# A four-layer hybrid decoder step: the residual chunks' scaled copy dropped, the first stage reordered, the final norm taken in feature layout

## The reference, cut to what matters

```python
for i in range(DEPTH):                       # mixers: gated MLP, linear attention, block attention, gated MLP
    x = x + mixer_i(rms_norm(x, norm_mix[i]))
    x = x + swiglu(rms_norm(x, norm_ffn[i]), w_up[i], w_down[i])
y = rms_norm(x, norm_final)

def rms_norm(x, g):
    return x * rsqrt(mean(x * x, axis=-1) + EPS) * g
```

## Time and profile before

| | |
|---|---|
| median of 3 runs | 1685.19 us (1681.47 to 1689.21) |
| profiled execution's own time | 1688.18 us |
| its span | 1686.4 us |
| PE busy | 1568.3 us, 93% |
| DVE busy | 1122.1 us, 67% |
| ACT busy | 794.2 us, 47% |
| mean granted TensorE clock | 0.972 of full |

### The profile page before, as it was taken

The page is one execution under the profiler, slowest core; times in us unless marked ns, Lnnn a source line. Parts: engine busy times, 40 slices in busy tenths (PEclk is TensorE's granted clock), DMA queues, the critical chain, the costliest instruction groups (busy, mean ns, idle before and its releaser), DMA issues.

```text
span 1686.4 us, 33530 instructions
## 1 busy us (share of the span) xinstructions
PE 1568.3 (93%) x12471; PEld 1517.4 (90%) x12471; DVE 1122.1 (67%) x1691; ACT 794.2 (47%) x1279; POOL 174.1 (10%) x168
## 2 busy tenths in 40 slices
PE   6999999999989779999987589999999999999995
PEld 5999999999879569999977459999999999999995
DVE  5578757665665867676557955666666786676643
ACT  4566445444435545444333345444355754354432
POOL 1000010000311400000126400000210001200000
PEclk9999999999999979999999799999999999999998
DMA  5454555554535724554578643555554445555551
GB/s 182 153 172 131 173 176 176 188 184 163 176 125 197 232 84 163 186 174 163 201 253 309 228 152 103 190 181 169 180 189 162 150 153 186 177 175 176 188 174 61
DMA packets 265123, 293.19 MB, mean 174 GB/s; under 512 B 6108, under 2 KB 256276, under 8 KB 265022
## 3 DMA queue, kind: packets, MB, share of 16 engines
q1 hardware_dynamic: 260252, 278.04, 49.3%
q0 software_dynamic: 4192, 13.66, 2.4%
q10 hardware_dynamic: 578, 0.08, 0.0%
HBM read 283.51 MB, written 8.25 MB: 173 GB/s over the span
## 4 chain that ended last, share of the span: by engine, by line
PE 71%; DVE 12%; DMA 5%; ACT 4%; issue 4%; POOL 1%; SPq 1%; DVEq 1%; ACTq 0%; POOLq 0%
PE banks L471 22%; PE banks L473 21%; PE banks L475 21%; DVE wlo L445 4%; ACT whi L437 2%; DMA raw<-in_w_down 2%; DVE xl L593 1%; DVE xg L587 1%; PE banks L958 1%; DMA raw<-in_w_in_c 1%; PE banks L1448 1%; DVE x L579 1%; DMA raw<-in_w_in_a 1%; DVE sc L1919 1%; PE banks L949 1%
## 5 line engine op out<-in xcount | busy, mean ns | idle before, releaser
L445 DVE TENSOR_TENSOR wlo<-raw,whi 128x1024 fp32r<-128x1024 f32 (+1 forms) x480 | 604.5, 1265 | 328.9 <-ACT whi L437 328.6
L437 ACT ACTIVATE whi<-raw 128x1024 fp32r<-128x1024 f32 (+1 forms) x480 | 498.0, 1044 | 648.0 <-PE banks L475 531.7
L471 PE MATMUL banks<-xh,whi 128*128 128x264 f32 x2560 | 744.7, 291 | 18.8 <-DVE xl L593 18.2
L473 PE MATMUL banks<-xl,whi 128*128 128x264 f32 x2560 | 729.4, 285 | 0.0
L475 PE MATMUL banks<-xh,wlo 128*128 128x264 f32 x2560 | 728.7, 285 | 0.0
L471 PEld LDWEIGHTS banks<-xh,whi 128*128 128x128 f32 x2560 | 486.8, 190 | 24.3 <-DVE xl L593 21.0
L473 PEld LDWEIGHTS banks<-xl,whi 128*128 128x128 f32 x2560 | 487.1, 190 | 0.9 <-issue 0.5
L475 PEld LDWEIGHTS banks<-xh,wlo 128*128 128x128 f32 x2560 | 484.2, 189 | 0.0
L471 PE MATMUL banks<-acth,whi 128*128 128x264 f32 x1216 | 348.7, 287 | 10.3 <-DVE actl L1577 10.3
L473 PE MATMUL banks<-actl,whi 128*128 128x264 f32 x1216 | 347.2, 286 | 0.0
L475 PE MATMUL banks<-acth,wlo 128*128 128x264 f32 x1216 | 346.6, 285 | 0.0
(11 more groups left out here) (289 smaller groups left out, 1168.1 us busy)
## 6 DMA issues: line engine op xcount, KB each, us to landing
raw<-in_w_up SPq DMA_DIRECT2D x88, 1024.0 KB, 4.9
raw<-in_w_in_a SPq DMA_DIRECT2D x48, 1024.0 KB, 5.1
raw<-in_w_down SPq DMA_DIRECT2D x32, 1024.0 KB, 4.7
raw<-in_w_out_a SPq DMA_DIRECT2D x24, 1024.0 KB, 4.7
raw<-in_w_down SPq DMA_DIRECT2D x16, 768.0 KB, 4.1
raw<-in_w_in_b SPq DMA_DIRECT2D x12, 1024.0 KB, 4.9
raw<-in_w_in_c SPq DMA_DIRECT2D x12, 1024.0 KB, 6.4
raw<-in_w_out_b SPq DMA_DIRECT2D x4, 1024.0 KB, 4.9
```

The lines of the kernel that those rows point to most:

```text
L437: act.activation(whi[:, slot, 0:k, side], raw[:, slot, 0:k, side], ACT.Copy)\
L445: dve.tensor_tensor(wlo[:, slot, 0:k, side], raw[:, slot, 0:k, side], whi[:, slot, 0:k, side].bitcast(F32), ALU.subtract)\
L471: pe.matmul(bank[:, 0:TOK], whi[:, slot, c, side], rh[:, c0 + c, :], start=(c0 + c == 0), stop=False)
L473: pe.matmul(bank[:, 0:TOK], whi[:, slot, c, side], rl[:, c0 + c, :], start=False, stop=False)
```

## The change

1. `xg` is dropped in all stages. ACT makes `xh` straight from `x` with the gain as the scale of its copy; DVE makes `xl = x * gain - xh` in one SCALAR_TENSOR_TENSOR. The two loops of every `out` and `down` stage on DVE and ACT are written out.
2. First stage: the chunks come ahead of the weight residues. ACT's two splits of piece 0 stand behind chunks 3 and 5, DVE's behind chunk 4 and after all chunks, and the eight squares of the first norm go behind the splits of piece 1. The final gain becomes 8 more rows of `col_rows` (one more transfer in front of the tokens).
3. Last `down` stage: DVE writes `xs = x * gain_final` and adds up the squares that ACT makes of each chunk; ACT loads the table of the root ahead of the stage.
4. Last stage: PE transposes `xs` into four PSUM banks (and two for the samples) and sums the squares per token with six pairs of one-column matmuls; the root and the inverse are taken of [128, 2] and [8, 1]; DVE and ACT each scale one block of 128 tokens from PSUM into `yout`; SP stores.

```diff
-        xg = sb("xg", [P, 2, TOK])
...
-        def new_chunk_vector(dve, norm, gain, m, j, tile, tile_wait, add):
+        def new_chunk_vector(dve, m, j, tile_wait, add):
...
-            need(dve, xl_done, DC * norm + m - 1)
-            dve.wait_ge(bank_read, tile + 1)
-            dve.tensor_scalar(xg[:, j % 2, :], chunk(x, m),
-                              cols[:, one(m + gain)], None, ALU.mult).then_inc(gained, 1)
...
+        def new_chunk_lo(dve, norm, gain, m):
 
             dve.wait_ge(xh_done, DC * norm + m + 1)
...
+            dve.scalar_tensor_tensor(out=xl[:, m, :], in0=x[:, m, :], scalar=cols[:, gain + m:gain + m + 1],
+                                     in1=xh[:, m, :].bitcast(F32), op0=ALU.mult, op1=ALU.subtract)\
+                .then_inc(xl_done, 1)
+
+        def new_chunk_scalar(act, gain, m, tile):
+
+            act.wait_ge(bank_read, tile + 1)
+            act.activation(xh[:, m, :], x[:, m, :], ACT.Copy, scale=cols[:, gain + m:gain + m + 1])\
                 .then_inc(xh_done, 1)
...
-            if norm is None:
-                body(0, False)
-                body(1, True)
-            else:
-                run_loop(dve, 0, 2, lambda i, f: body(i, False))
+            for i in range(2):
+                body(i, norm is None and i == 1)
...
+                            if has_norm(name):
+                                new_chunk_scalar(act, gain_of(name), m, at["tile"] + m)
+                            else:
+                                act.wait_ge(bank_read, at["tile"] + m + 1)
+                                act.activation(x_sq[:, m, :], x[:, m, :], ACT.Square).then_inc(x_sq_done, 1)
...
+                act.activation(small[:, 12:13], eps[:, :], ACT.Sqrt)
...
         def vector_load(dve):
             dve.memset(eps[:, :], EPS).then_inc(ones_done, 1)
             dve.memset(ones[:, :], 1.0).then_inc(ones_done, 1)
-            for half in range(2):
-                split_lo(dve, half + 1, 0, half, KC)
             dve.wait_ge(cols_turned, 1)
...
             for m in range(DC):
-                new_chunk_vector(dve, 0, 0, m, m, m, (tile_made, m + 1), False)
+                new_chunk_vector(dve, m, m, (tile_made, m + 1), False)
                 if m:
-                    new_chunk_lo(dve, 0, m - 1, m - 1)
-            new_chunk_lo(dve, 0, DC - 1, DC - 1)
+                    new_chunk_lo(dve, 0, 0, m - 1)
+                if m == 4:
+                    split_lo(dve, 1, 0, 0, KC)
+            new_chunk_lo(dve, 0, 0, DC - 1)
+            split_lo(dve, 2, 0, 1, KC)
             for half in range(2):
                 split_lo(dve, half + 3, 1, half, KC)
...
         def scalar_load(act):
-            for half in range(2):
-                split_hi(act, 16, 0, 0, half, KC)
+            act.wait_ge(cols_done, 1)
             for m in range(DC):
                 new_chunk_scalar(act, 0, m, m)
-                act.activation(x_sq[:, m, :], x[:, m, :], ACT.Square).then_inc(x_sq_done, 1)
+                if m in (3, 5):
+                    split_hi(act, 16, 0, 0, m // 4, KC)
             for half in range(2):
                 split_hi(act, 16, 0, 1, half, KC)
+                for m in range(4 * half, 4 * half + 4):
+                    act.activation(x_sq[:, m, :], x[:, m, :], ACT.Square).then_inc(x_sq_done, 1)
...
+        def scaled_chunk(dve, m):
+
+            dve.wait_ge(bank_read, LAST + m + 1)
+            dve.tensor_scalar(xs[:, m, :], x[:, m, :], cols[:, COLS - DC + m:COLS - DC + m + 1], None, ALU.mult)\
+                .then_inc(xs_done, 1)
+            if m >= 2:
+                dve.wait_ge(x_sq_done, FINAL_SQ + m)
+                if m > 2:
+                    dve.wait_ge(fin_summed, m - 2)
+                dve.tensor_tensor(sqsum[:, :], x_sq[:, 0, :] if m == 2 else sqsum[:, :], x_sq[:, m - 1, :],
+                                  ALU.add).then_inc(fin_summed, 1)
+
         def pe_final(pe):
...
+            pe.wait_ge(bank_read, LAST + 6)
+            for c in range(DC):
+                if c == 6:
+                    pe.wait_ge(bank_read, LAST + 7)
+                    pe.wait_ge(fin_summed, DC - 2)
+                    pe.wait_ge(x_sq_done, FINAL_SQ + DC)
+                    for b in range(NBLK + 1):
+                        n, side = (P, slice(b * P, b * P + P)) if b < NBLK else (NSAMP, slice(SEQ, TOK))
+                        pe.matmul(ps[2][0:n, b:b + 1], sqsum[:, side], ones[:, 0:1], start=True, stop=False,
+                                  skip_group_check=True)
+                        mm = pe.matmul(ps[2][0:n, b:b + 1], x_sq[:, DC - 1, side], ones[:, 0:1], start=False,
+                                       stop=True, skip_group_check=True)
+                    mm.then_inc(fin_squared, 1)
+                pe.wait_ge(xs_done, c + 1)
+                side = slice(c % 4 * P, c % 4 * P + P)
                 for b in range(NBLK):
...
+                    pe.transpose(ps[4 + 2 * b + c // 4][:, side], xs[:, c, b * P:(b + 1) * P], ident[:, :])
+                pe.transpose(ps[c // 4][0:NSAMP, side], xs[:, c, SEQ:TOK], ident[:, :]).then_inc(tile_made, 1)
...
+            dve.tensor_scalar(yout[:, 1, :], allps[:, 6:8, :].rearrange("p e d -> p (e d)"), small[:, 9:10], None,
+                              ALU.mult).then_inc(y_done, 1)
...
+            act.activation(yout[:, 0, :], allps[:, 4:6, :].rearrange("p e d -> p (e d)"), ACT.Copy,
+                           scale=small[:, 8:9]).then_inc(ya_done, 1)
...
+        def sp_final(sp):
+
+            for b, done in enumerate((ya_done, y_done)):
+                sp.wait_ge(done, 1)
+                sp.dma_start(A["y_prompt"][0, b * P:(b + 1) * P, :], yout[:, b, :]).then_inc(y_stored, 16)
+            sp.wait_ge(ya_done, 2)
+            sp.wait_ge(y_done, 2)
```

More of the change, by code:

```diff
@@ L623, in body @@
                         if whole:
-                            new_chunk_vector(dve, norm, gain_of(name), 4 * i + j, j,
-                                             at["tile"] + 4 * i + j,
-                                             (mm_done, mm_value(name, i, j)), True)
+                            new_chunk_vector(dve, 4 * i + j, j, (mm_done, mm_value(name, i, j)), True)
+                            if norm is None:
+                                scaled_chunk(dve, 4 * i + j)
                         if half == 0:
@@ L649, in body @@
                             split_next(act, name, i, t, half, last)
[L650 to L655, removed]
+                        if t % (per // 2) == per // 2 - 1:
+                            m = 4 * i + 2 * (t // (per // 2)) + half
+                            if has_norm(name):
[3 more added lines that the diff above has]
+                                act.activation(x_sq[:, m, :], x[:, m, :], ACT.Square).then_inc(x_sq_done, 1)
+                            if has_norm(name) and at["norm"] in SQUARED:
+                                act.activation(x_sq[:, m, :], x[:, m, :], ACT.Square).then_inc(x_sq_done, 1)
                         if half == 1:
@@ L659, in scalar_out @@
             if not has_norm(name):
[L660 to L663, removed]
+                act.activation(small[:, 12:13], eps[:, :], ACT.Sqrt)
+            for i in range(2):
+                body(i, i == 1 and not has_norm(name))
         def pool_squares(pool, name):
@@ L1242, in scalar_sgu @@
                 highs += 1
-        def pe_final(pe):
-            at = ph["final"]["tile"]
-            for m in range(DC):
-                pe.wait_ge(bank_read, at + m - BANKS + 1)
-                pe.wait_ge(bank_read, ph[("down", DEPTH - 1)]["tile"] + m + 1)
-                bank = ps[m % BANKS]
-                for b in range(NBLK):
-                    pe.transpose(bank[:, b * P:(b + 1) * P], x[:, m, b * P:(b + 1) * P], ident[:, :])
-                pe.transpose(bank[0:NSAMP, SEQ:SEQ + P], x[:, m, SEQ:TOK], ident[:, :])\
-                    .then_inc(tile_made, 1)
@@ L1281, in scalar_final @@
-        def scalar_final(act):
-            act.wait_ge(bank_read, ph["final"]["tile"] + DC)
-            act.wait_ge(y_done, DC)
-            for b in range(NBLK + 1):
-                n = P if b < NBLK else NSAMP
-                act.activation(yout[0:n, b, :], ytok[0:n, b, :], ACT.Square,
-                               accum_out=small[0:n, b:b + 1]).then_inc(fsq_done, 1)
-            for b in range(NBLK + 1):
-                n = P if b < NBLK else NSAMP
-                act.wait_ge(fsq_done, b + 1)
-                act.activation(small[0:n, 4 + b:5 + b], small[0:n, b:b + 1], ACT.Sqrt,
-                               scale=1.0 / D, bias=eps[0:n, :]).then_inc(fstd_done, 1)
@@ L1294, in pool_final @@
-        def pool_final(pool):
-            for b in range(NBLK):
-                pool.wait_ge(y_done, DC + b + 1)
-                store(pool, A["y_prompt"][0, b * P:(b + 1) * P, :], yout[:, b, :])
-            pool.wait_ge(y_done, DC + NBLK + 1)
-            store(pool, A["y_sample"].rearrange("b s d -> (b s) d"), yout[0:NSAMP, NBLK, :])
```

(4 more changed lines are left out.)

94 lines of the change are left out of this document (42 added, 52 removed).

## The result

| | before | after |
|---|---|---|
| median | 1683.55 us (1680.76 to 1689.21, 6 runs) | 1657.39 us (1654.46 to 1662.13, 6 runs) |
| profiled execution, its span | 1688.18 us, 1686.4 us | 1654.46 us, 1652.7 us |
| PE busy | 1568.3 us, 93% | 1564.3 us, 95% |
| mean granted TensorE clock | 0.972 | 0.979 |

The ratio is 0.9846, 95% interval 0.9831 to 0.9861: 26.2 us faster. Rival C had the time nearest to it (1661.8), but not for its reasons, as will be seen.

A forecast was written before the change was run, and what follows sets the result against it. TensorE is busy 93% of the span, so only time around its matmuls can be won: start 1.6, boundaries 9, end 6.2, sum 16.8; 1685.19 - 16.8 = 1668.4 us, range 1660 to 1678.

The forecast's parts named there:

- Rival C: Whole kernel: everything shifts, no clock lost at start, stores land in 3.1; 23.4 us gained, 1661.8; chance 0.13.
- The 3.75 behind the last landing stay: Program end: the 3.75 us from the last store's landing to the span's end stay unchanged; the end gains 6.2.
- The unrolled loops I cost at nothing: Stage loops on DVE: writing them out costs nothing, as DVE has no gap there that a wait does not explain.
- the 9 of the sum: Seven stage boundaries: dropping `xg` gains 10.35 us, less 1.4 for a slower `xl`, taken as 9.
- Into layer 2, where the weight piece is late, only the last chain is shortened: 1.0: Boundary from layer 1's `down` into layer 2: behind a late weight piece, dropping `xg` gains only 1.0 us.
- The 1.35 that I took off for a slower `xl`: Seven boundaries: `xl` beside POOL's squares more often, 0.2 us each, 1.4; 10.35 was taken as 9.
- The loss of clock that I took off: First stage: PE's pause for the moved squares may lower the clock, costing 1.5 us; start gain taken as 1.6.
- B: Boundaries give little: the next wait stands behind the vanished one and the clock falls; 10.3 us gained, 1674.9; chance 0.22.
- D: Boundaries yield nothing, weight transfers set the pace, the squares' wait eats the start; only the end gains; 1678.5; chance 0.08.
- E: Slower: written-out loops fetched anew, 3.5 us at each of seven boundaries, 24.5 against 16.8; 1692.9; chance 0.04.
- the port's lock passes to `xl` and the residues: Boundaries: squares now start beside `xl` and weight residues, taking back about 0.5 at four boundaries, 2 us of 10.35.

## Why the prediction was too small

The gain was 26.2 where the sum had 16.8. Of the 9.4 that are missing, 4.4 stand at the end, 4.4 in the middle and 0.6 at the start.

**"The 3.75 behind the last landing stay": the step that failed at the end.** From the last landing to the end of the span I took a constant of the program. It held only where POOL waits for the stores; with SP waiting it was 1.87. The landing was mis-sized as well: I had 5.1 from the first issue to the last landing, and all of SP's end, from the first issue to the end of the span, took 4.8, of which an estimate of 2.9 is left for the landing (4.8 - 1.87). So my sum described the kernel with its stores on POOL, whose end took 14.0 against a forecast of 14.1. The sum had a gain of 6.2 for the end, it measured 10.6. The working up to the stores was near: roots at 1645.93, 2.9 behind the last `x` (forecast 3.0), the first store at 1647.94, 4.9 behind it (forecast 5.3 by the numbers of the sum).

**"The unrolled loops I cost at nothing": the step that failed in the middle, and half-hidden by the other edit.** The reason given was that DVE has no idle time at its loops that a wait does not explain. That is true and beside the point: the 50 ns of register work show as an `xg` of 0.81 instead of 0.36, a duration and not a gap. Alone the loops are worth 12.5 us. Beside the dropped `xg` they buy only what `xl` loses in them (794 against 648 ns) and the shorter chain, some 2.5 to 4 us, because both edits take away the same waits of PE. With the loops kept, the middle gained 9.5 by the medians (13.4 - 3.9), near the 9 of the sum: what was missing in the middle is about what the loops add, as far as the noise of 5 us lets one say it. Had I costed each edit alone and added them, I would have had 22 (12.5 + 9.5) for the middle, 8.6 too much where 9 was 4.4 too little. I had seen the symptom (the earlier trace rows has the 0.81) and read it as the cost of `xg` itself.

**"Into layer 2, where the weight piece is late, only the last chain is shortened: 1.0": the most mis-sized of the boundaries that do not lie in a noisy stretch.** It measured 3.6, and 2.6 with the loops kept (198.1 us for the stretch). I held the piece's lateness fixed. ACT's waits for weight pieces, before and after, in the 60 us up to that boundary (800 to 860 and 787 to 846):

```profile
ACT whi L437 <- DMA raw<-in_w_down: 12.0, 4, 5.7
ACT whi L437 <- DMA raw<-in_w_in_c: 11.6, 2, 6.9
```

```profile
ACT whi L439 <- DMA raw<-in_w_in_c: 8.8, 2, 5.6
...
ACT whi L439 <- DMA raw<-in_w_down: 7.3, 2, 3.9
```

A slot is loaded again only when DVE has made both residues of the piece in it, and every `xg` that DVE made or was held up in lay ahead of a residue. So the delay travels through the transfer to the next piece, and taking it away brings the piece forward too. Over the span ACT's waits for `w_down` pieces fell from 38.5 to 21.0 us, for `w_out_a` from 17.6 to 5.0. That this link and not the shorter work at the boundary carries the extra 2.6 us (3.6 - 1.0) fits these rows, but no run isolates it. The other boundaries that do not lie in a noisy stretch came near: 3.9 against 3.8 where the earlier trace rows were read, clock of 1.00 included; 2.9 against 2.15; 1.3 and 0.8 against 0.5 each. The 1.35 that I took off for a slower `xl` did not come due: `xl` rose by 26 ns a chunk, 1.7 us over all 64, mostly off PE's path.

**The start: 2.2 against 1.6.** At equal landing of the tokens it is 1.8, and nearly all of it is the missing `xg`, not the order. The wait was foreseen rightly (PE waits for the moved squares, 1.65 measured, 1.9 to 3.9 forecast). The loss of clock that I took off did not happen at 1.65 us, nor at 1.67, 1.78, 1.79 and 2.81 in other runs; it did at 2.04 and 2.51, where the 16 passes took 5.51 and 5.35 instead of 3.83. So the fear had its ground, and the length of the wait alone does not decide: the clock held behind 2.81. Not foreseen was the table load of 1.28 us ahead of ACT's first copy; before, it lay at 3.30 to 4.58, in ACT's idle time ahead of the first weight piece. It was made up for by tokens that landed at 8.73 where I had 9.9, so that the sum's end (27.4 forecast, 27.59 measured) came out nearly right by luck: two errors met. The Trainium skill (ScalarE: Activation LUTs, What ACT_TABLE_LOAD costs) gives about 1.283 us for the load alone, and the trace agrees with 1.28.

**The rivals.** B and D (less at the boundaries) are out: 13.4 there, against B's 3.5. C reached nearly the time, by "the stores land in 3.1", which is not what happened: its end was 7.6 and not 10.6, though its middle of 13 was right. E is refuted by the run with the loops alone: where it wanted a loss of 24.5 us for written-out code, that code alone gained 12.5. What the prediction drew from the Trainium skill (SBUF — State Buffer, Who interferes with whom), that the port's lock passes to `xl` and the residues, was true in the rows: beside POOL's squares and sums an `xl` of 0.98 and a residue of 1.60, where 0.5 and 1.23 are usual. It cost little in the time: PE's waits for `xl` fell to 4.3 all the same.

## What to carry to other kernels

Before costing two edits, ask whether they take away the same wait, and read long durations beside another engine's start times and not only idle times: 50 ns ahead of an instruction cost it 0.45 us here, 28 times. Where a buffer is released by the delayed engine, a wait at its transfer is not a constant. And look at which engine issues and which awaits the last stores: moving both from POOL to SP gave 4 us for nothing.

## What was not expected of the hardware

- A `TENSOR_SCALAR` of DVE recorded 30 to 50 ns ahead of POOL's square took 0.81 or 0.82 us (28 of them), one recorded 50 to 160 ns ahead 0.36 (52, in two kernels).
- Stores issued by POOL left 2.0 us more to the end of the span than SP's (5.77 against 3.8), and a final wait on POOL another 1.9 (7.65). The Trainium skill (DMA: Bandwidth & Descriptors, Latency and other measured facts) has SyncE's first byte about 0.4 us sooner; the direction agrees, the end of the program shows more.
- ACT's copy of 128x264 took 0.51 us with a column of gains as its scale and 0.42 without; it adds 0.09 to the path of each `xh`.
- The spread of one kernel's runs goes with the granted clock (0.979 at 1654.46, 0.973 at 1662.13). Between two traces of one code it lay in the stretches of two mixers: 192.5 and 191.4 us in one, 197.8 and 187.1 in the other.
